# Attention in two stages: block products for every projection with queries and gates kept in DRAM, then 64 softmax units

## What is computed

```python
# h: normed main sequence (512), hc: normed context (256), both 1024 wide
q, k, v, g = split(h @ w_in)          # 16 query heads, 8 key and 8 value heads, 16 gates, each 128 wide
_, kc, vc, _ = split(hc @ w_in)       # of the context only keys and values are used
q, k = rope2d(rmsnorm(q, q_g)), rope2d(rmsnorm(k, k_g))     # kc is normed, but not rotated
k_all, v_all = concat(kc, k), concat(vc, v)                  # 768 keys
o = softmax(q @ k_all.T * 128 ** -0.5) @ v_all               # two query heads share one key head
x = x + gate * ((o * silu(g)) @ w_out)
```

## Time and profile before

| | before |
|---|---|
| median of 3 runs | 4115.13 us (4114.27 to 4117.16) |
| the profiled execution | 4119.65 us, its span 4117.8 us |
| granted PE clock, mean over the span | 0.985 |
| PE busy | 3873.4 us, 94% of the span |
| DVE busy | 2212.9 us, 54% |
| ACT busy | 955.8 us, 23% |
| POOL busy | 992.8 us, 24% |
| DMA | 320.05 MB, 78 GB/s over the span |
| grouped attention, first projection to first product of `attn_out` | 3075.45 to 3724.66 us of the span |

### The profile page before, as it was taken

One profiled execution on the slowest core, in us unless ns is written; L12 is line 12 of the kernel. 1 busy time (PEld: TensorE's weight loads), 2 busy tenths in 40 slices (PEclk: granted clock), 3 DMA queues, 4 the chain that ended last, 5 costly groups with the idle time before them and its releaser, 6 DMA issues. The chain is left out here.

```text
span 4117.8 us, 75565 instructions
## 1 busy us (share of the span) xinstructions
PE 3873.4 (94%) x33254; PEld 2703.5 (66%) x33254; DVE 2212.9 (54%) x3428; ACT 955.8 (23%) x1755; POOL 992.8 (24%) x749
## 2 busy tenths in 40 slices
PE   6999999999999999999998888888899999999997
PEld 3488888758888855555555777787655555557443
DVE  2577725668785149836443455555424444453693
ACT  1411100110110020021014444444213444441102
POOL 0144544104444420001332223322010001014200
PEclk9999999999999999999999999999999999999998
DMA  2133323423442212112324211110201111111221
GB/s 72 57 113 140 106 83 129 167 112 123 143 143 82 72 51 61 41 41 77 108 93 165 96 35 35 39 49 17 82 31 59 57 44 54 57 39 52 72 72 41
DMA packets 152192, 320.05 MB, mean 78 GB/s; under 512 B 15936, under 2 KB 111168, under 8 KB 141120
## 3 DMA queue, kind: packets, MB, share of 16 engines
q1 hardware_dynamic: 148144, 304.81, 21.8%
q0 software_dynamic: 3728, 10.49, 1.0%
HBM read 277.52 MB, written 30.41 MB: 75 GB/s over the span
## 5 line engine op out<-in xcount | busy, mean ns | idle before, releaser
L931 PE MATMUL lin_ps<-hn,ring 128*128 128x256 f32 (+1 forms) x3968 | 1272.5, 476 | 20.5 <-ACT arena L1876 9.1
L931 PEld LDWEIGHTS lin_ps<-hn,ring 128*128 128x128 f32 x3968 | 750.3, 190 | 493.1 <-issue 431.9
L931 PE MATMUL lin_ps<-arena 64*64 64x64 f32 (+5 forms) x9784 | 701.6, 258 | 78.0 <-ACT arena L1876 32.7
L931 PE MATMUL lin_ps<-arena,ring 128*128 128x256 f32 (+1 forms) x2784 | 705.0, 409 | 11.2 <-DVE arena L2928 7.6
L931 PEld LDWEIGHTS lin_ps<-arena 64*64 64x64 f32 (+2 forms) x9784 | 532.2, 144 | 177.0 <-issue 94.7
L931 PEld LDWEIGHTS lin_ps<-arena,ring 128*128 128x128 f32 x2784 | 531.6, 192 | 154.5 <-issue 82.5
L1876 ACT ACTIVATE arena<-lin_ps 128x512 f32<-128x512 f32 (+3 forms) x491 | 248.2, 527 | 913.3 <-PE lin_ps L931 881.9
L2472 DVE SCALAR_TENSOR_TENSOR arena<-arena,vec 128x512 f32<-128x512 f32 (+3 forms) x499 | 392.6, 861 | 1.3
L2472 DVE SCALAR_TENSOR_TENSOR arena<-arena,cs 128x512 f32<-128x512 f32 x336 | 345.3, 1095 | 0.0
L931 PE MATMUL sum_ps<-arena 64*64 64x64 f32 (+1 forms) x7176 | 309.7, 224 | 21.9 <-issue 14.1
L931 PEld LDWEIGHTS sum_ps<-arena 64*64 64x64 f32 (+1 forms) x7176 | 261.2, 137 | 36.3 <-issue 22.4
(11 more groups left out here) (253 smaller groups left out, 4564.8 us busy)
## 6 DMA issues: line engine op xcount, KB each, us to landing
ring<-w_up SPq DMA_DIRECT2D x32, 1024.0 KB, 5.8
ring<-w_down SPq DMA_DIRECT2D x32, 1024.0 KB, 5.0
arena<-w_mod SPq DMA_DIRECT2D x24, 1024.0 KB, 7.7
arena<-w_mod SPq DMA_DIRECT2D x12, 2048.0 KB, 7.8
features<-arena SPq DMA_DIRECT2D x64, 384.0 KB, 6.2
ring<-w_attn SPq DMA_DIRECT2D x16, 1536.0 KB, 6.6
ring<-w_conv_in SPq DMA_DIRECT2D x16, 1024.0 KB, 5.7
ring<-features SPq DMA_DIRECT2D x40, 384.0 KB, 3.4
```

What stands on the lines that cost most here:

```text
L931: return pe.matmul(out, lhsT, rhs, start=start, stop=stop)
```

## The change

The grouped attention is cut into two stages.

**Stage one, `attn_p`**: all projections are 24 pairs of block products of 1 MB of weights each, in the order `kv0 q0 kv1 q1 kv2 q2 g0 kv3 q3 g1 ... kv7 q7 g5 g6 g7`: key and value of one key head, the two queries, the two gates. Before each kv pair stands `context(n)`, the keys and values of the context as 16 plain products of 256 columns. Behind pair n stands what pair n-1 needs (`beside_pair`). Keys and values of all eight rounds stay in SBUF. Queries, once rotated, and gates, once through Silu, are stored to DRAM by SP (`keep_made`), 512 KB a pair: two buffers `made_q`, one buffer `made_g`. DVE does `normalize(n-2)`, `take_pair` of pair n, `rotated(n-2)`; POOL does `weight_sums` of chunk n, then the swaps of pair n-3.

**Stage two**: 64 units with nothing beside them. Scores have two buffers and probabilities three. `turn(U-2)` stands behind `scores(U)`, and the weighing of a head is cut in four parts of 2, 2, 1 and 1 products over the units U = 4h+6 to 4h+9. DVE divides unit U-1 behind the maximum of unit U, and does `head_out` of head h at U = 4h+10. SP loads one head's queries and one head's gates at a time (256 KB each, two buffers of each), in one queue: head h+1's queries behind head h's gates. POOL forms the sums of the first two chunks of `attn_out` at the start of stage two, instead of one early and one after the last head.

```diff
-    ("attn", 16, 3072, 0, ()),
...
+           ("rw_r2", 2, 1), ("rw_k", 4, 1), ("rw_v", 4, 1), ("rw_g", 4, 1), ("attn_p", 24, 1), ("attn_out", 4, 2)]
...
+ATTN_ORDER = ["kv0", "q0", "kv1", "q1"]
+for _r in range(2, 8):
+    ATTN_ORDER += [f"kv{_r}", f"q{_r}", f"g{_r - 2}"]
+ATTN_ORDER += ["g6", "g7"]
+ATTN_TASKS = []
+for _n, _name in enumerate(ATTN_ORDER):
+    if _name[0] == "k":
+        ATTN_TASKS.append(("ctx", int(_name[2])))
+    if _n:
+        _last, _r = ATTN_ORDER[_n - 1][0], int(ATTN_ORDER[_n - 1][-1])
+        ATTN_TASKS += [(t_, _r) for t_ in {"k": ("sks", "skc", "va", "vb"), "q": ("sq0", "sq1"), "g": ()}[_last]]
...
-        return (n + 1 + (n >= CHUNK0)) % 3
+        return (n + 1 + (n >= CHUNK0) + (n >= CHUNK1)) % 3
...
+        ak, av = [at(ALL * r, ALL) for r in range(8)], [at(6144 + ALL * r, KB, P) for r in range(8)]
...
+        head_q, head_g = [at(20480 + SEQ * b, SEQ) for b in range(2)], [at(21504 + SEQ * b, SEQ) for b in range(2)]
+        made_q, made_g = [at(22528 + 1024 * b, 2, SEQ) for b in range(2)], at(24576, 2, SEQ)
...
+        probs = [std[:, :], rstd[:, :], at(22528, ALL)]
+        task_ps = [sum_ps[:, 0:512], sum_ps[:, 512:1024], out_ps[:, 0, :], out_ps[:, 1, :]]
+        score_ps = [lin_ps[:, b, 256:1024] for b in range(2)]
...
+            def keep_made(n):
+
+                name, r = ATTN_ORDER[n], int(ATTN_ORDER[n][-1])
+                f, sem_ = (0, q_stored) if name[0] == "q" else (1, g_stored)
+                if name[0] == "q":
+                    sp.wait_ge(qk_ready, 3 * r + 3)
+                else:
+                    sp.wait_ge(gated_g, USED + r + 1)
+                if r:
+                    sp.wait_ge(sem_, USED + 16 * r)
+                to = scratch[2 * f + 2 * r // KD, 2 * r % KD:2 * r % KD + 2, :, 0:SEQ].rearrange("a p n -> p a n")
+                sp.dma_start(to, made(name)).then_inc(sem_, 16)
...
+                        elif name == "attn_p":
+                            key, r = ATTN_ORDER[step][0], int(ATTN_ORDER[step][-1])
+                            lo = {"k": 0, "q": 0, "g": P}[key]
+                            w = t["w_attn"][2 * r + (key != "q"), :, :].rearrange("p (k n) -> p k n", k=KD)[:, :, lo:lo + (P if key == "k" else 256)]
+                            to = raw_slot(n).rearrange("p (k n) -> p k n", k=KD)
+                            if key == "k":
+                                k = t["w_attn"][2 * r, :, :].rearrange("p (k n) -> p k n", k=KD)[:, :, 256:384]
+                                sp.dma_start(to[:, :, 0:P], k).then_inc(raw_full[raw_turn(n)], 16)
+                                to = to[:, :, P:256]
...
+                        if name == "attn_p":
+                            for n_ in (step - 4, step - 5):
+                                if n_ >= 0 and ATTN_ORDER[n_][0] == ("q" if n_ == step - 5 else "g"):
+                                    keep_made(n_)
...
+                if name == "attn":
+                    first, last = Q["attn_p"].chunk1, len(ATTN_ORDER)
+                    for step in range(last, last + 5):
+                        for n_ in (step - 4, step - 5):
+                            if n_ < last and ATTN_ORDER[n_][0] == ("q" if n_ == step - 5 else "g"):
+                                keep_made(n_)
+                    for h in range(HEADS):
+                        sp.wait_ge(q_stored, USED + 16 * (h // 2 + 1))
+                        if h >= 2:
+                            sp.wait_ge(sc_mm, QB * (h - 1))
+                        sp.dma_start(head_q[h % 2], kept(0, h)).then_inc(q_in[h % 2], 16)
+                        sp.wait_ge(g_stored, USED + 16 * (h // 2 + 1))
+                        if h >= 2:
+                            sp.wait_ge(hd_ev, h - 1)
+                        sp.dma_start(head_g[h % 2], kept(1, h)).then_inc(g_in[h % 2], 16)
...
+                lead = early and name in ("up0", "up1", "sgu_u", "attn_p")
...
                 n = task_no(r, name)
-                pe.wait_ge(pj_ev, max(n - 1, 0))
-                return task_ps[n % 2]
...
+                pe.wait_ge(pj_ev, max(n - 3, 0))
+                return task_ps[n % 4]
...
+            def context(n):
+
+                r, c = int(ATTN_ORDER[n][2]), Q["attn_p"].chunk0 + n
+                pe.wait_ge(raw_full[raw_turn(c)], raw_count(c))
+                to = take_bank(r, "ctx")
+                w = raw_slot(c).rearrange("p (k n) -> p k n", k=KD)
+                for v in range(2):
+                    for k in range(KD):
+                        if n == 0 and v == 0:
+                            pe.wait_ge(h_ready, 8 * NI["at"] + k + 1)
+                        m = mm(to[:, CTX * v:CTX * v + CTX], w[:, k, P * v:P * v + P], hn[:, k, 0:CTX], k == 0, k == KD - 1)
+                m.then_inc(pj_mm, 1)
...
+            def beside_pair(n):
+
+                key, r = ATTN_ORDER[n][0], int(ATTN_ORDER[n][-1])
+                if key == "k":
+                    square_sum(r, "sks", 1, aksq[:, CTX:ALL])
+                    square_sum(r, "skc", 1, aksq[:, 0:CTX])
+                    pe.wait_ge(pj_ev, task_no(r, "ctx") + 1)
+                    pe.wait_ge(bank_ev, bank_free(Q["attn_p"].pair0 + n + 1))
+                    turn_v(r, "va", range(2, KB))
+                    turn_v(r, "vb", range(2))
+                if key == "q":
+                    square_sum(r, "sq0", 2, asq[:, 0, :])
+                    square_sum(r, "sq1", 3, asq[:, 1, :])
...
+            for n in range(len(ATTN_ORDER)):
+                if ATTN_ORDER[n][0] == "k":
+                    context(n)
+                pair_products("attn_p", n, 0, attn_p_b, attn_p_need)
+                if n:
+                    beside_pair(n - 1)
...
+
+                h, q = U // QB, U % QB
+                if q == 0:
+                    pe.wait_ge(qk_ready, 3 * (h // 2) + 1)
+                    pe.wait_ge(q_in[h % 2], USED + 16 * (h // 2 + 1))
+                pe.wait_ge(sc_ev, max(U - 1, 0))
...
+            pe.wait_ge(bank_ev, bank_free(Q["attn_p"].pair1))
...
+                if 2 <= U < UNITS + 2:
+                    turn(U - 2)
+                if U >= 6:
+                    weigh((U - 6) // QB, [(0, 1), (2, 3), (4,), (5,)][(U - 6) % QB])
             pe.wait_ge(sc_ev, UNITS)
...
+            def made_pair(n):
+
+                key, r = ATTN_ORDER[n][0], int(ATTN_ORDER[n][-1])
+                act.wait_ge(bank_ev, bank_free(Q["attn_p"].pair0 + n + 1))
+                if key == "k":
+                    act.wait_ge(pj_ev, task_no(r, "ctx") + 1)
+                    f(aksq, ak[r], ACT.Square).then_inc(pj_sq, 1)
+                if key == "q":
+                    for h in range(2):
+                        f(asq[:, h, :], made(ATTN_ORDER[n])[:, h, :], ACT.Square).then_inc(pj_sq, 1)
+                if key == "g":
+                    f(made_g, made_g, ACT.Silu).then_inc(gated_g, 1)
...
+                if key == "k":
+                    if r:
+                        act.wait_ge(qk_norm, 3 * r - 2)
                     mean_root(r, "sks", akstd[:, CTX:ALL])
                     mean_root(r, "skc", akstd[:, 0:CTX])
-                if i == 4 and part == 1:
-                    take(r, "vs", avT[:, CTX:ALL], ACT.Copy)
-                if i == 5 and part == 0:
+                    take(r, "va", av[r][:, 2:KB, :].rearrange("p a b -> p (a b)"), ACT.Copy)
+                    take(r, "vb", av[r][:, 0:2, :].rearrange("p a b -> p (a b)"), ACT.Copy)
...
+            for U in range(UNITS + 2):
+                if U >= 2:
+                    take_turned(U - 2)
+                if U < UNITS:
+                    exps(U)
...
+            def normalize(n):
+
+                key, r = ATTN_ORDER[n][0], int(ATTN_ORDER[n][-1])
+                if key == "k":
+                    dve.wait_ge(pj_ev, task_no(r, "skc") + 1)
+                    o(nc.vector.reciprocal(akstd, akstd))
+                    o.wait()
+                    o(stt(ak[r], ak[r], V("attn_k_g_2", 0), akstd, ALU.mult, ALU.mult), normed)
...
+            def attn_pair(n):
+
+                key, r = ATTN_ORDER[n][0], int(ATTN_ORDER[n][-1])
+                if key == "k":
+                    top, low = ak[r][:, CTX:ALL], avT[:, r % 2, CTX:ALL]
+                    if r >= 2:
+                        dve.wait_ge(pj_mm, task_no(r - 2, "vb") + 1)
+                else:
+                    top, low = made(ATTN_ORDER[n])[:, 0, :], made(ATTN_ORDER[n])[:, 1, :]
+                    if key == "q" and r >= 2:
+                        dve.wait_ge(q_stored, USED + 16 * (r - 1))
+                    if key == "g" and r:
+                        dve.wait_ge(g_stored, USED + 16 * r)
+                b = Q["attn_p"]
+                take_pair(b.pair0 + n, b.chunk(n, 0) + 1, (top[:, lo_t], top[:, hi_t]), (low[:, lo_t], low[:, hi_t]))
+
+            for n in range(len(ATTN_ORDER)):
+                if n >= 2:
+                    normalize(n - 2)
+                attn_pair(n)
+                if n >= 2:
+                    rotated(n - 2)
...
```

(34 more changed lines are left out.)

336 lines of the change are left out of this document (113 added, 223 removed).

## The result

The changed kernel took 4075.84 us (median of 4 runs, 4067.3 to 4077.33) beside 4116.15 us (4114.27 to 4126.69) for the kernel before on the same chip: ratio 0.9888, 95% interval 0.9874 to 0.9901. By that ratio it is some 46 us less, by the two medians 40.3. Forecast were 46.4 less, 4069 us, 4048 to 4096; the median is 6.8 us above the forecast. The profiled execution took 4077.33 us, with a span of 4075.5.

What follows compares the result with a forecast made beforehand. PE's instructions and waits were taken as the bound: 581.8 - 4 + 2 + 10 + 2 + 4 + 7 = 602.8 us against 649.2, 46.4 less. That made the forecast 4069 us, range 4048 to 4096.

Steps and rivals of the forecast that it cites:

- PE's work: Both stages: PE's instructions take 581.8 us, with block pairs of 12.09 instead of 13.74 us saving 39.6.
- Start: Before the first context product: the 2.0 us wait and 2 us of low clock go, -4 us.
- VectorE and GpSimd in stage one: Stage one: their work stays under PE's 46.9 us period; 2 us charged for odd waits, bounds 0 and 24.
- rival (d): Stage one: DVE and POOL hold it up by common SBUF access, 4091 to 4100 us; chance 0.12.
- The join: Between stages: PE waits 10 us for head 0's queries, loaded behind the store of g7; bounds 6 and 15.
- Low clock and fill: Start of stage two: low clock behind the gap +2 us, filling the pipe +4, bounds 2 and 6.
- Units: Stage two: turning U-2 hides the division, so no wait charged; bounds 0 and 0.65 us a unit.
- rival (e): Stage two: units stay bound by their chain, 0.65 us each, 42 in all, 4111 us; chance 0.04.
- Head loads: Stage two: queries behind gates land 0.5 us late for each of 14 heads, +7 us, bounds 0 and 49.
- (c): Stage two: late head queries cost more, landing in 3.7 to 5 us, 4076 to 4094 us; chance 0.14.
- (f): Stage two: queries landing in over 6.6 us at each head make the kernel slower, 4121 at 7; chance 0.08.
- Rival (b): Both stages: everything hidden, loads in time, join 6 us, nothing in stage one, 4054 us; chance 0.18.

Runs made afterwards that it cites:

- e4: Changed kernel with the last block product formed twice in 23 stage-one pairs, 32 products a pair: 4108.13 us, ratio 0.9974 to the kernel before.
- e7: Changed kernel with the first pair's context products waiting for all eight normed tiles instead of one by one: 4076.36 us, run once.
- e10: Changed kernel with GpSimd forming weight sums of stage-one pairs 1 to 23 for 4 of 128 columns only: 4065.27 us, ratio 0.9881 to the kernel before.
- e1: Changed kernel with SP issuing head h+1's queries ahead of head h's gates in stage two: 4064.84 us.
- e0: The changed kernel again, unedited, as base for the edits: 4072.43 us beside 4120.72 for the kernel before, ratio 0.988.
- e8: Changed kernel with one more VectorE reciprocal of 352 columns behind each of the 24 stage-one pairs: 4078.43 us, stage one 15.7 us longer.
- e9: Changed kernel with two more VectorE reciprocals of 352 columns behind each stage-one pair: 4121.2 us, stage one 51.4 us longer.
- e2: Changed kernel with queries and gates of heads 0 and 1 loaded before the last stores of stage one: 4064.88 us.
- e3: Changed kernel with the edits of e1 and e2 together: 4051.9 us, ratio 0.9831 to the kernel before.
- e11: As e5, but VectorE divides unit U-1 ahead of the maximum of unit U: 4072.45 us, ratio 0.9894 to the kernel before.
- e5: Changed kernel with stage two turning the unit before (U-1) instead of U-2: 4281.27 us, stage two 214 us longer.

## Why the prediction was right, and where it was not, point by point

- **PE's work, 581.8 us, of it 39.6 saved by the block form:** right. Stage one is 375.1 us against 374.6 + 2, and e4 gives 39.5 back with 23 of the 24 pairs, 1.72 us each where the sum has 1.65.
- **Start, -4:** both parts are real, 2.25 of wait and 1.74 of clock (e7). But the sum took the second off twice: the 581.8 are counted at full clock and never held it. The term should have been -2.
- **VectorE and GpSimd in stage one, +2, and rival (d):** the time was right; d falls by e10, by 0.2 us. Of the estimate, VectorE's 29 us alone measured 28.0, and 37 beside GpSimd measured 34.5. The Trainium skill, SBUF — State Buffer, section "SBUF: two separate sides", has the shared port pair as an exclusive lock, taken for the whole instruction by the one that starts first. That both lose where both read SBUF agrees with the rows: GpSimd's sums go from 1.26 to 1.5 or 1.6 us on average, and a rotation step grows by 0.85, less than the 1.26 of a whole sum, so the wait seen is mostly a part of one instruction. VectorE's reciprocals and its additions from PSUM lose nothing; its division in stage two does (e1). What I did not see is that the cover is uneven: it is 12.5 us in a steady period and 2.5 in the third stretch (e0), and the swap's way through GpSimd and DMA has to fit as well (e8, e9).
- **The join, +10:** the mechanism was right, head 0's queries behind the last store (e2). The term was mis-sized: it measured 5.56. The store of g6 landed at 3451.1, 2.3 us ahead of the end of the last pair and not behind it, because the two stores of 512 KB issued at 3446.95 took 2.8 and 3.7 us where I had taken 6.2 from the earlier trace rows. So the additions ended 0.45 us behind PE instead of 3 to 4; Silu, the issues and the load, which landed in 3.5, are the other 5.1.
- **Low clock and fill, +2 and +4:** together right. From the first scores to the first weighing is 18.7 us in e0 (3457.28 to 3475.97) for 12.3 of work, 6.4 more (seven scores of 1.29 and five turns of 0.66 are 12.3); without the gap it is 4.5 (e2), and without GpSimd's sums in the fill 2.4 (e3). By that the clock was 1.9 and the fill 4.5. That GpSimd's sums for attn_out would slow the division of the first units was not among my steps.
- **Units, 0, and rival (e):** right for the kernel as it is, 12.96 us for four units with no wait. But the reason was half wrong. I took 3.9 us from the earlier trace rows as the length of the unit's chain; that row held the next unit's maximum, put ahead of the division. Alone the chain is 3.1 (e11). Given VectorE's order as it stands, turning two units later is worth 214 us (e5), with the division first 9, and that beside heads whose lateness takes 8.5 back (e11).
- **Head loads, +7:** right, 8.4 in e0 (0.6 a head where 0.5 was forecast), because SP's queue has the queries behind the gates (e1), and not by the landing, 2.9 us for 256 KB. Behind the size some luck stands: scores want the queries 2.7 us after their issue (2.75 forecast), and the median landing of 2.9 in place of the 3.2 would make a head only 0.2 late. The rest are single landings of 3.3 and 3.6, 0.1 us from landing to scores, and 0.08 by which the first scores run slower. Rivals (c) and (f) would have needed landings of 3.7 and over 6.6. The Trainium skill, DMA: Bandwidth & Descriptors, section "Anatomy of one DMA", gives its 2.0 us and bytes over 436 GB/s for DMAs that GpSimd issues, and SyncE issues these. Taken over all the same, its 2.6 us are an estimate 0.3 short of the median, and would have had no head late.
- **The sum:** with the slip at the start put right it is 604.8 against 649.2, 44.4 less; measured were 666.5 - 619.1 = 47.4. The misses: stage one -1.5, gap -4.4, stage two +3.1 (223.3 against 207.2 + 2 + 4 + 7), the start -0.15. So the forecast of 46.4 came so near by luck in part: a gap taken for too long worked against a term taken off twice and a stage two taken for too short. The profiled pair differs by 42.3 us only, since the part ahead of the attention was 5.0 us longer in that execution (last norm sum at 3063.12 against 3058.17), with the same code. That scatter, up to 12 us, is large enough for the 6.8 us between forecast and median as well.

Rival (b), everything hidden, is what e3 comes to by two edits in SP's queue.

## What to carry to other kernels

Where one engine has all the work of a stage, count its instructions; then go through every wait that the reordering makes and ask in which queue it stands: both losses left here (8.4 us at the heads, 6.9 at the join) were a load standing in an in-order queue behind something it did not need, and went by issuing the same loads in another order. Before you credit a deeper pipeline, look at the order of work on the engine between its two ends: a maximum ahead of a division made one unit of distance cost 214 us, behind it 9. A small difference can be a balance, too: those 9 are losses of 18 and a gain of 8.5. And test cover by adding work, stage by stage: an average slack of 12 us of 47 hid stretches with 2.5.

## What the runs showed of the hardware that I had not expected

- GpSimd's sums doubled VectorE's division of 768 columns by a column of scalars (0.62 to 1.22 us), which has only one large input, but neither the maximum over PSUM (0.96 in both) nor the reciprocals.
- The clock fell behind PE gaps of 2.1 us (0.59 for 4 us, e7), 3.0 us (0.61, e8) and 5.6 us (0.50, then 0.65), not behind one of 0.52 (e2). But the length alone does not tell it: waits of 1.5 to 2.35 us in e9 and of 2.32 in e8 left it at 1.00 (16 products in 3.69 us behind each), and so did waits of 1.8 us in the fill of e11 (1.00 from 3454.74 to 3462.74, with PE busy 2.2 of 4 us). No run shows what makes the difference.
- In e5 it stayed low on average, 0.81, through 436 us of units with a wait of some 2.2 us each. There the waits cost about half as much again as their own length: 138 us of waits, some 76 more.
- Behind the same gap of 5.6 us the clock was back sooner in e1 (0.67 and 0.91 in the windows where e0 has 0.50 and 0.69). No run tells why.
